# A hybrid decoder trunk in split float32: the order of work at the begin of gate and up, and the outer products of the state update a slab later

## The chip, the cores and the metric

One Trainium2 chip, one core. The metric is device microseconds of one launch, lower is better. Engines are named PE (TensorE), DVE (VectorE), ACT (ScalarE), POOL (GpSimd) and SP (SyncE, which here only issues DMAs).

## What is computed

Two layers (D_MODEL 1024, 512 prompt tokens and 8 sample tokens side by side, float32). Each layer is a mixer and a SwiGLU feed-forward:

```python
h = h + _rmsnorm(m, norm_mix_post[l])
f = _swiglu(_rmsnorm(h, norm_ffn_pre[l]), w_gate_up[l], w_down[l])
h = h + _rmsnorm(f, norm_ffn_post[l])

def _swiglu(hn, w_gate_up, w_down):
    gu = hn @ w_gate_up
    gate, up = jnp.split(gu, 2, axis=-1)
    return (jax.nn.silu(gate) * up) @ w_down
```

The mixer also updates a 128 x 128 state per head for each sample token: new state = decayed state + outer product of key and value (four DeltaNet and four retention heads, 8 sample tokens).

## The kernel before

**Precision.** Each float32 product is done as three products of tensors split in a rounded part (`Xh`, `Wh`, `actH`, made by ACT, `hi`) and a rest (`Xl`, `Wl`, `actL`, made by DVE as the difference, `lo`). 520 columns (two halves of 256 prompt and 4 sample tokens) lie in two PSUM banks; a pair of banks is a slot.

**Weights** come as slabs of eight 128 x 128 blocks (512 KB) over SP's queue into two `stage` buffers, and are split into three `Wh`/`Wl` buffers. A slab is loaded when the `lo` of two slabs before is done; ACT's `hi` of a slab waits until PE has finished with the one three before.

**Gate and up.** The first five of 22 column blocks of gate and up are ten plain tiles (`T_GU` + 0 to 9; even ones gate, odd ones up; `mm6`, L676), one slab each. Tiles `T_GU` + 0 to 2 are computed interleaved in `first_halves`, the others in a row. A tile starts on PE when its slab is split (`wait_slab`) and the tile two before it has been evacuated by DVE (`wait_tile`, semaphores `tile_free0` and `tile_free1`). DVE's loop over j = 0 to 4 evacuates the gate tile (`gp`, L2476), then the up tile (`up`, L2493), scaling both by the norm's factor `rb`; ACT applies SiLU to `gp` between (L1764); then DVE multiplies (L2496). `lo` of a coming slab stands behind each evacuation.

The other 17 column blocks (`Q`) are done by `strassen(q)`: a 2 x 2 scheme with seven products (`UN`) in place of eight, over four blocks of 128 each, with three matmuls per block and product (L1231 to L1233), 84 in all. It needs
- the activations once per layer: `weighted(k)` (ACT, L1706, eight times, two at a time into `XF`), `x_scaled(0..3)` (DVE, L2389, times `rb`), `x_sum(0..3)` (DVE, L2397), `x_high(0..6)` (ACT, L1710), `x_low(0..6)` (DVE, L2401);
- a set of weights per q (`loC`/`hiC`/`fullC` for q = 0, then B and A in turns): four quarters of 256 KB by SP (`quarters`, into `raw12`, `raw1`, `raw21`), `w_sums13`, `w_sum2`, `w_sum4` and four rests `w_low` (DVE), four roundings `w_high` (ACT). Rest 12 (`W_LO12`) is the last that the first product `UA11` waits for, `W_LO46` is waited for by the fifth, `US3`, which also waits for `post(q, U2)` (L2443), one of five small DVE steps that combine products.

These steps were spread by hand over DVE's and ACT's loops of the ten tiles. The scalings 0 and 1 stand at the end of j = 0, ahead of the evacuation of tile `T_GU` + 2; 2 and 3 stand in j = 1 ahead of the evacuation of `T_GU` + 3; the set for q = 0 is made in j = 4 and behind it. Nearly all of these steps count up one semaphore, `ffn_rest`, in program order.

**Down.** 22 slabs, eight tiles of 22 blocks each. After slab 0 PE transposes keys and values of the sample tokens back to rows (`rows_back`); DVE copies them (L2568, L2569) and builds 16 value blocks (`value_block(u)`, L2369); PE makes the outer product `outer(u)` (L1197) after a slab; DVE adds it to the decayed state (`new_state(u)`), which POOL has loaded into one of two `dst` buffers and stores afterwards (`load_state`, `store_state`, in POOL's queue in order). Every engine works its queue in order; what is written behind a wait waits with it.

Of the kernel before, what the change touches and what calls it, by code (L numbers as in the profile page):

```python
# [8 lines left out]
def trunk(nc, xT, w_slabs, w_ba, w_rows, dt_bias, a_log, conv_hist, state_gdn, state_ret, c_f32, c_rope,  # L9
# [7 lines left out]
    P = 128  # L17
# [52 lines left out]
    X_STEPS, XR_STEPS = 8 + UN, KT + UN  # L70
    REST, ROUND = X_STEPS + Q * W_STEPS, XR_STEPS + Q * 4

# [27 lines left out]
    with ctx:  # L100
# [285 lines left out]
        def heads_of(i):  # L386
# [22 lines left out]

            "b1_loaded b12_loaded b21_loaded p_done post_done ffn_rest ffn_round gate_half "  # L410

# [68 lines left out]
        def _(sp):  # L480
# [14 lines left out]
            def quarters(l, q):  # L495

                N = l * Q + q
                used = l * REST + X_STEPS + (q - 1) * W_STEPS
                if q == 0:
                    sp.wait_ge(s["rb_ready"], (l * 4 + 3) * 2)  # L500
                else:
                    sp.wait_ge(s["ffn_rest"], used + W_T13)
                sp.dma_start(raw12[:], quarter(l, q, 1, 0)).then_inc(s["b12_loaded"], 16)
                if q == 0:
                    sp.wait_ge(s["dr_mm"], (l + 1) * 16)
                else:
                    sp.wait_ge(s["ffn_rest"], used + W_LO05)
                sp.dma_start(raw1[:, 0], quarter(l, q, 0, 0)).then_inc(s["b1_loaded"], 16)
                sp.dma_start(raw1[:, 1], quarter(l, q, 1, 1)).then_inc(s["b1_loaded"], 16)
                if q == 0:  # L510
                    last = S_DN - 1 - (l * SLABS + S_DN - 1 - (NW - 1)) % NW
                    sp.wait_ge(s["tile_done"], l * TILES + T_GU + last - S_GU + 1)
                else:
                    sp.wait_ge(s["ffn_rest"], used + W_LO3)
                sp.dma_start(raw21[:], quarter(l, q, 0, 1)).then_inc(s["b21_loaded"], 16)
# [65 lines left out]
        def _(pool):  # L581
# [13 lines left out]
            for l in range(DEPTH):  # L595
# [59 lines left out]
                pool.wait_ge(s["dr_mm"], (l + 1) * 16)  # L655
                pool.wait_ge(s["ffn_rest"], l * REST + X_STEPS + (Q - 1) * W_STEPS + W_LO05)
                load_state(l, 0, False)
# [12 lines left out]
        def _(pe):  # L670
# [53 lines left out]
            for l in range(DEPTH):  # L724
# [474 lines left out]
                def strassen(q):  # L1199
# [4 lines left out]
                    for u, bank in enumerate((a_, b_, c_, a_, b_, c_, d_)):  # L1204
                        if q == 0:
                            pe.wait_ge(s["ffn_rest"], l * REST + 8 + u + 1)
                        if u == UA11:
                            pe.wait_ge(s["ffn_rest"], l * REST + X_STEPS + q * W_STEPS + W_LO12)
                            if q == 0:
# [8 lines left out]
                        elif u == US1 and q >= 2:  # L1218
                            pe.wait_ge(s["post_done"], (N - 2) * POSTS + C12)
                        elif u == UA12:  # L1220
                            pe.wait_ge(s["gate_half"], N * HALVES + P1_COPY)
                        elif u == US3:
                            pe.wait_ge(s["ffn_rest"], l * REST + X_STEPS + q * W_STEPS + W_LO46)
# [32 lines left out]
                for i in range(KT - 1):  # L1256
                    wait_tile(l, T_DN + i)
                    for j in range(FT):
# [36 lines left out]
        def _(act):  # L1295
# [16 lines left out]
            for l in range(DEPTH):  # L1312
# [395 lines left out]
                def x_high(u):  # L1708
                    act.wait_ge(s["ffn_rest"], l * REST + (1, 7, 5, 4, 6, 8, 4)[u])
                    A(XU[:, u, 0], x_full(u), ACT.Copy).then_inc(s["ffn_round"], 1)  # L1710

                def w_high(q, c):

                    N = l * Q + q
                    lo_, hi_, full = w_set(q)
                    rest = l * REST + X_STEPS + q * W_STEPS
                    if c == W_HI05:
# [5 lines left out]
                    elif c == W_HI12:  # L1723
                        act.wait_ge(s["ffn_rest"], rest + W_T2)
                        to, src = hi_[:, US2:US1 + 1], full[:, US2:US1 + 1]
                    else:
                        act.wait_ge(s["ffn_rest"], rest + W_T4)
                        to, src = hi_[:, US3:UA22 + 1:2], full[:, US3:UA22 + 1:2]
# [31 lines left out]
                for j in range(NP):  # L1760
# [101 lines left out]
        def _(dve):  # L1862
# [12 lines left out]
            for l in range(DEPTH):  # L1875
# [508 lines left out]
                def x_scaled(i):  # L2384
# [3 lines left out]
                    dve.wait_ge(s["ffn_round"], l * ROUND + (4 if i < 2 else KT))  # L2388
                    V.tensor_tensor(to, to, rb[:, a:a + 1].to_broadcast([P, 4, HC]), ALU.mult).then_inc(s["ffn_rest"], 1)  # L2389

                def x_sum(i):
# [3 lines left out]
                                          (US2, x_full(US1), x_full(UA11), ALU.subtract, 5), (US4, x_full(UA12), x_full(US2), ALU.add, 7))[i]  # L2395
                    dve.wait_ge(s["ffn_rest"], l * REST + need)
                    V.tensor_tensor(x_full(to), x, y, op).then_inc(s["ffn_rest"], 1)  # L2397

                def x_low(u):
                    dve.wait_ge(s["ffn_round"], l * ROUND + KT + u + 1)  # L2400
                    V.tensor_tensor(XU[:, u, 1], x_full(u), plain(XU[:, u, 0]), ALU.subtract).then_inc(s["ffn_rest"], 1)  # L2401

                def w_sums13(q):
# [4 lines left out]
                    dve.wait_ge(s["b1_loaded"], (N + 1) * 32)  # L2408
                    V.tensor_tensor(full[:, US1:US3 + 1:2], raw1[:], raw12[:].unsqueeze(1).to_broadcast([P, 2, QW]), ALU.add).then_inc(s["ffn_rest"], 1)

                def w_sum2(q):
                    full = w_set(q)[2]
                    dve.wait_ge(s["ffn_rest"], l * REST + X_STEPS + q * W_STEPS + W_T13)
                    V.tensor_tensor(full[:, US2], full[:, US1], raw1[:, 1], ALU.add).then_inc(s["ffn_rest"], 1)

                def w_sum4(q):
                    full = w_set(q)[2]
                    dve.wait_ge(s["b21_loaded"], (l * Q + q + 1) * 16)
                    dve.wait_ge(s["ffn_rest"], l * REST + X_STEPS + q * W_STEPS + W_T2)
                    V.tensor_tensor(full[:, UA22], full[:, US2], raw21[:], ALU.add).then_inc(s["ffn_rest"], 1)  # L2420

                def w_low(q, c):
# [5 lines left out]
                    else:  # L2428
                        us = slice(US2, US1 + 1) if c == W_HI12 else slice(US3, UA22 + 1, 2)
                        src = full[:, us]  # L2430
                        dve.wait_ge(s["ffn_rest"], l * REST + X_STEPS + q * W_STEPS + W_T4)
                    dve.wait_ge(s["ffn_round"], l * ROUND + XR_STEPS + q * 4 + c)
                    V.tensor_tensor(lo_[:, us], src, plain(hi_[:, us]), ALU.subtract).then_inc(s["ffn_rest"], 1)

# [37 lines left out]
                for j in range(NP):  # L2472
# [91 lines left out]
                for i in range(KT * FT // 8 - NW):  # L2564
                    lo(G0 + S_DN + i + NW)
                    if i == 1:
                        dve.wait_ge(s["row_T"], l + 1)
                        step.go(V.tensor_copy(flat2(krows[:]), PS[0:3 * H * NB, 6, 0:2 * P]))  # L2568
                        step(V.tensor_copy(flat2(vrows[:]), PS[0:3 * H * NB, 6, 2 * P:4 * P]))  # L2569
                    if 1 <= i < 17:  # L2570
                        value_block(i - 1)
                    for k in range(KT - 2):
                        if (FT * k + FT - 1) // 8 == i:
                            down_tile(k)
                    if 2 <= i < 18:
                        new_state(i - 2)
                down_tile(KT - 2)
# [146 lines left out]
```

## Time and profile before

| | |
|---|---|
| median of 3 runs | 1404.09 us (1403.06 to 1404.29) |
| profiled execution | 1401.79 us, span 1400.0 us |
| PE busy | 1366.9 us (98%), 12172 matmuls |
| DVE busy | 1040.2 us (74%) |
| ACT busy | 634.9 us (45%) |
| POOL busy | 100.7 us (7%) |
| share of the chain that ended last | PE 83%, DVE 10%, ACT 3% |
| mean granted clock of PE | 0.996 |

Busy shares are averages over the whole span; what a reordering is worth is read from the single waits of PE, in the timeline. Times in the timelines count from the span's start. Durations of back-to-back matmuls overlap, so the start of the next is the better clock for PE, as it is for DVE. Layer 1 repeats layer 0 some 695.2 us later.

### The profile page before, as it was taken

How to read it: one execution, taken by the hardware profiler on the slowest of the kernel's cores; microseconds unless marked ns; L12 is line 12 of the kernel's file. 1: busy time of each engine (PE TensorE's matmuls, PEld its weight loads, DVE VectorE, ACT ScalarE, POOL GpSimd, SP SyncE). 2: the span in 40 equal slices, each digit the busy share in tenths (PEclk: the TensorE clock that was granted, in tenths of full speed). 3: DMA queues.
4: the chain of work that ended last, by engine and by line, in shares of the span. 5: the costliest groups of instructions: out<-in, count | busy, mean ns of one | idle time of the engine just before them, and what ended most of it. 6: DMA issues, size and time to landing. Idle time of an engine off the chain costs nothing.

```text
span 1400.0 us, 29086 instructions
## 1 busy us (share of the span) xinstructions
PE 1366.9 (98%) x12172; PEld 1343.3 (96%) x12172; DVE 1040.2 (74%) x1675; ACT 634.9 (45%) x1230; POOL 100.7 (7%) x141
## 2 busy tenths in 40 slices
PE   8999999999999999999999999999998999999997
PEld 8999999998999999999989999999988999999996
DVE  7746896867888888754586568958778888886554
ACT  5135554557445455422442364634574445454222
POOL 0001211000000000011000012210000000000110
PEclk9999999999999999999999999999999999999999
DMA  6322232022222322354313312421212232323552
GB/s 207 111 102 76 85 115 98 32 79 79 98 99 99 113 99 104 124 181 181 114 61 118 110 62 84 130 69 46 89 69 92 99 113 98 114 95 140 173 180 77
DMA packets 67491, 147.46 MB, mean 105 GB/s; under 512 B 20128, under 2 KB 23584, under 8 KB 67360
## 3 DMA queue, kind: packets, MB, share of 16 engines
q1 hardware_dynamic: 59536, 119.90, 25.2%
q0 software_dynamic: 7824, 25.70, 5.3%
q8 instruction: 96, 1.57, 0.5%
q14 instruction: 35, 0.29, 0.1%
HBM read 132.79 MB, written 12.78 MB: 104 GB/s over the span
## 4 chain that ended last, share of the span: by engine, by line
PE 83%; DVE 10%; ACT 3%; issue 2%; DMA 1%; SPq 0%; DVEq 0%; ACTq 0%
PE PS L676 43%; PE PS L1231 8%; PE PS L1232 8%; PE PS L1233 8%; PE PS L682 5%; DVE Wl L1873 2%; DVE hT L1911 1%; ACT Wh L1310 1%; DVE Xl L1890 1%; ACT XF L1706 1%; DVE actL L2467 1%; ACT actH L1756 1%; DVE mT L1910 1%; PE PS L870 1%; PE PS L1197 1%
## 5 line engine op out<-in xcount | busy, mean ns | idle before, releaser
L1310 ACT ACTIVATE Wh<-stage 128x1024 fp32r<-128x1024 f32 x143 | 151.0, 1058 | 327.1 <-PE PS L676 300.3
L676 PE MATMUL PS<-Xh,Wh 128*128 128x260 f32 x1376 | 285.7, 289 | 7.5 <-DVE sqb L2493 2.7
L676 PE MATMUL PS<-Xh,Wl 128*128 128x260 f32 x1376 | 276.9, 283 | 0.0
L676 PE MATMUL PS<-Xl,Wh 128*128 128x260 f32 x1376 | 276.5, 282 | 0.0
L1873 DVE TENSOR_TENSOR Wl<-stage,Wh 128x1024 fp32r<-128x1024 f32 x143 | 174.5, 1222 | 102.8 <-ACT Wh L1310 102.1
L676 PEld LDWEIGHTS PS<-Xh,Wh 128*128 128x128 f32 x1376 | 211.4, 189 | 11.6 <-issue 6.8
L676 PEld LDWEIGHTS PS<-Xh,Wl 128*128 128x128 f32 x1376 | 211.8, 188 | 0.0
L676 PEld LDWEIGHTS PS<-Xl,Wh 128*128 128x128 f32 x1376 | 211.7, 188 | 0.0
L1231 PE MATMUL PS<-XU,hiA 128*128 128x260 f32 x448 | 126.8, 283 | 0.0
L1231 PE MATMUL PS<-XU,hiB 128*128 128x260 f32 x448 | 126.8, 283 | 0.0
L1232 PE MATMUL PS<-XU,hiB 128*128 128x260 f32 x448 | 126.6, 283 | 0.0
L1232 PE MATMUL PS<-XU,hiA 128*128 128x260 f32 x448 | 126.6, 283 | 0.0
L1233 PE MATMUL PS<-XU,loB 128*128 128x260 f32 x448 | 126.4, 282 | 0.0
L1233 PE MATMUL PS<-XU,loA 128*128 128x260 f32 x448 | 126.4, 282 | 0.0
L676 PE MATMUL PS<-actH,Wh 128*128 128x260 f32 x616 | 124.0, 282 | 0.0
L676 PE MATMUL PS<-actL,Wh 128*128 128x260 f32 x616 | 124.0, 282 | 0.0
L676 PE MATMUL PS<-actH,Wl 128*128 128x260 f32 x616 | 123.9, 282 | 0.0
L676 PEld LDWEIGHTS PS<-actH,Wh 128*128 128x128 f32 x616 | 97.2, 188 | 1.4
L676 PEld LDWEIGHTS PS<-actL,Wh 128*128 128x128 f32 x616 | 94.8, 188 | 0.0
L676 PEld LDWEIGHTS PS<-actH,Wl 128*128 128x128 f32 x616 | 94.8, 188 | 0.0
L1232 PEld LDWEIGHTS PS<-XU,hiA 128*128 128x128 f32 x448 | 84.7, 189 | 0.0
L1232 PEld LDWEIGHTS PS<-XU,hiB 128*128 128x128 f32 x448 | 84.7, 189 | 0.0
(384 smaller groups left out, 2875.1 us busy)
## 6 DMA issues: line engine op xcount, KB each, us to landing
stage<-w_slabs SPq DMA_DIRECT2D x143, 512.0 KB, 3.3
raw<-w_slabs SPq DMA_DIRECT2D x136, 256.0 KB, 2.6
dst<-state_ret POOLq DMA_DIRECT2D x32, 256.0 KB, 3.6
dst<-state_gdn POOLq DMA_DIRECT2D x32, 256.0 KB, 3.8
out_gdn_sample<-dst POOLq DMA_DIRECT2D x16, 256.0 KB, 3.0
out_ret_sample<-dst POOLq DMA_DIRECT2D x16, 256.0 KB, 3.3
hT<-x_t SPq DMA_DIRECT2D x3, 520.0 KB, 6.6
out_y_t<-hT SPq DMA_DIRECT2D x3, 520.0 KB, 3.0
```

The source lines that it names most:

```text
L676: ins = mm(pj(slot)[:, a], w[:, ws, pos, :], x[:, a, :], start=first and w is Wh and x is xh, stop=last and w is Wl)
L682: ins = mm(pj(slot)[:, a], w[:, ws, pos, :], x[:, a, :], start=first and w is Wh and x is xh, stop=last and w is Wl)
L870: ins = mm(PS[rows, 7, B_U:B_U + P], vectors, dst[:, u % 2, j, :], start=n == 0, stop=n == 7 and u < 8, skip_group_check=True)
L1197: mm(PS[:, 4 + u % 2, :], krows[:, u // 8, :], vblks[u % 2].rearrange("p a n -> p (a n)"), start=True, stop=True).then_inc(s["outer_mm"], 1)
L1231: mm(PS[:, bank, 0:HC], hi_[:, u, cols], XU[:, u, 0, k], start=k == 0 and u in (UA11, US2, US1, UA22), stop=False, skip_group_check=True)
L1232: mm(PS[:, bank, 0:HC], hi_[:, u, cols], XU[:, u, 1, k], start=False, stop=False, skip_group_check=True)
L1233: ins = mm(PS[:, bank, 0:HC], lo_[:, u, cols], XU[:, u, 0, k], start=False, stop=k == 3, skip_group_check=True)
L1310: A(Wh[:, G % NW], stage[:, G % NS], ACT.Copy).then_inc(s["hi_split"], 1)
L1706: A(to, hT[:, k], ACT.Copy, scale=prm[:, l, row:row + 1]).then_inc(s["ffn_round"], 1)
L1756: A(actH[:, j:j + n], actF[:, j:j + n] if j < FT - 2 else act_full(j).unsqueeze(1), ACT.Copy).then_inc(s["ah_ready"], n)
L1873: V.tensor_tensor(Wl[:, G % NW], stage[:, G % NS], Wh[:, G % NW].bitcast(fp32), ALU.subtract).then_inc(s["lo_split"], 1)
L1890: V.scalar_tensor_tensor(Xl[:, k, a], hT[:, k, a], prm[:, layer, row:row + 1], Xh[:, k, a].bitcast(fp32), ALU.mult, ALU.subtract).then_inc ...
```

## The change

In gate and up, on DVE: `x_scaled(0)` and `(1)` move from the end of j = 0 to j = 1 behind the evacuation of tile `T_GU` + 2 (and `lo`); `x_scaled(2)` and `(3)` move behind the evacuation of `T_GU` + 3; sums and `x_low` follow later by about half a round. `w_sums13(0)` and `w_sum2(0)` move to the end of j = 3; the rests 05, 3 and 12, `w_sum4(0)` and `x_low(6)` move ahead of the evacuation of the last plain tile, only rest 46 stays behind it. On ACT: `w_high(0, W_HI05)` and `w_high(0, W_HI3)` with the wait for `state_stored` move from behind the loop into j = 3, behind `x_high`. As steps of activations and of weights are now interleaved in another order, `ffn_rest` is split into `xu_rest` (activations) and `w_rest` (weights), with the counts adapted at every wait, SP's and POOL's too. In down, row copies, value blocks, outer products and state additions come one slab later.

```diff
-    REST, ROUND = X_STEPS + Q * W_STEPS, XR_STEPS + Q * 4
+    REST, ROUND = Q * W_STEPS, XR_STEPS + Q * 4
...
-                        elif b % 8 == 7 and 2 <= b // 8 < 18:
-                            outer(b // 8 - 2)
+                        elif b % 8 == 7 and 3 <= b // 8 < 19:
+                            outer(b // 8 - 3)
...
                     if j == 3:
                         for u in range(3, UN):
                             x_high(u)
-                act.wait_ge(s["state_stored"], (l + 1) * 32)
-                for c in range(W_HI05, W_HI46 + 1):
-                    w_high(0, c)
+                        act.wait_ge(s["state_stored"], (l + 1) * 32)
+                        w_high(0, W_HI05)
+                        w_high(0, W_HI3)
+                w_high(0, W_HI12)
+                w_high(0, W_HI46)
...
                     if j == 1:
-                        x_scaled(2)
-                        x_scaled(3)
+                        x_scaled(0)
+                        x_scaled(1)
                     elif j == 2:
+                        x_sum(1)
                         x_sum(2)
-                        x_sum(3)
                     elif j == 3:
                         x_low(2)
                         x_low(3)
                     elif j == 4:
-                        w_sums13(0)
-                        w_sum2(0)
                         w_low(0, W_HI05)
+                        w_sum4(0)
+                        w_low(0, W_HI3)
+                        w_low(0, W_HI12)
+                        x_low(6)
                     done(t + 1)
                     freed(V.tensor_tensor(up, pj(1), rb[:], ALU.mult), t + 1)
...
-                    if j == 0:
-                        x_scaled(0)
-                        x_scaled(1)
-                    elif j == 1:
+                    if j == 1:
+                        x_scaled(2)
+                        x_scaled(3)
                         x_sum(0)
-                        x_sum(1)
                     elif j == 2:
+                        x_sum(3)
                         x_low(0)
                         x_low(1)
                     elif j == 3:
-                        for u in range(4, UN):
-                            x_low(u)
+                        x_low(4)
+                        x_low(5)
+                        w_sums13(0)
+                        w_sum2(0)
                     elif j == 4:
-                        w_sum4(0)
-                        w_low(0, W_HI3)
-                        w_low(0, W_HI12)
                         w_low(0, W_HI46)
...
-                    if i == 1:
+                    if i == 2:
                         dve.wait_ge(s["row_T"], l + 1)
...
-                    if 1 <= i < 17:
-                        value_block(i - 1)
+                    if 2 <= i < 18:
+                        value_block(i - 2)
...
-                    if 2 <= i < 18:
-                        new_state(i - 2)
+                    if 3 <= i < 19:
+                        new_state(i - 3)
```

## Rows read from the trace of the kernel before

**Rows 1.** Waits of PE, whole run: who waited for whom, us in total, times, longest

```profile
PE PS L1231 <- DVE loC L2433: 7.8, 2, 3.9
PE PS L676 <- DVE sqb L2493: 2.7, 4, 1.2
PE PS L676 <- DVE sqb L2476: 2.2, 2, 1.1
...
PE PS L1197 <- DVE vblk L2369: 0.8, 2, 0.4
```

**Rows 2.** Timeline of PE: start us, us, engine, line, operation [idle before <- releaser]

```profile
341.10 0.48 PE L676 MATMUL PS<-Xh,Wh 128*128 128x260 f32 x2 [0.20 <-DVE sqb L2493]
...
348.18 0.47 PE L676 MATMUL PS<-Xh,Wh 128*128 128x260 f32 x2 [1.12 <-DVE sqb L2476]
...
355.32 0.47 PE L676 MATMUL PS<-Xh,Wh 128*128 128x260 f32 x2 [1.17 <-DVE sqb L2493]
```

**Rows 3.** Timeline of PE, from the last plain tile to the third Strassen block

```profile
383.95 0.40 PE L676 MATMUL PS<-Xh,Wl 128*128 128x260 f32 x2
388.26 0.56 PE L1231 MATMUL PS<-XU,hiC 128*128 128x260 f32 x1 [3.91 <-DVE loC L2433]
...
399.85 0.29 PE L1231 MATMUL PS<-XU,hiB 128*128 128x260 f32 x1
...
409.95 0.29 PE L1231 MATMUL PS<-XU,hiA 128*128 128x260 f32 x1
```

**Rows 4.** Stretches: length, busy us of PE, PEld, DVE, ACT, POOL, PEclk, DMA share, GB/s

```profile
384.40:388.26 3.86, 0.00 (x0) 0.03 (x1) 3.83 (x6) 1.80 (x2) 0.00 (x0) 0.95 0.17 55
388.26:391.40 3.14, 3.14 (x15) 3.14 (x16) 3.11 (x4) 0.36 (x2) 0.00 (x0) 0.52 0.20 78
1083.40:1087.60 4.20, 4.20 (x22) 4.20 (x23) 3.99 (x4) 2.04 (x4) 0.00 (x0) 0.60 0.33 117
```

**Rows 5.** Timeline of DVE at the first plain tiles of layer 0

```profile
345.03 2.39 DVE L2389 TENSOR_TENSOR XF<-XF,rb 128x1040 f32<-128x1040 f32 x2 [1.26 <-ACT XF L1706]
347.35 0.69 DVE L2476 TENSOR_TENSOR sqb<-PS,rb 128x520 f32<-128x520 f32 x1
...
352.17 2.39 DVE L2389 TENSOR_TENSOR XF<-XF,rb 128x1040 f32<-128x1040 f32 x2 [3.00 <-ACT XF L1706]
354.48 0.69 DVE L2493 TENSOR_TENSOR sqb<-PS,rb 128x520 f32<-128x520 f32 x1
```

**Rows 6.** Timeline of DVE behind the last plain tile of layer 0

```profile
384.39 0.70 DVE L2493 TENSOR_TENSOR sqb<-PS,rb 128x520 f32<-128x520 f32 x1 [2.08 <-PE PS L676]
385.12 0.70 DVE L2496 TENSOR_TENSOR actF<-sqb 128x520 f32<-128x520 f32 x1
385.74 0.68 DVE L2420 TENSOR_TENSOR fullC<-fullC,raw 128x512 f32<-128x512 f32 x1
...
386.94 2.35 DVE L2433 TENSOR_TENSOR loC<-fullC,hiC 128x1024 fp32r<-128x1024 f32 x2
389.21 1.22 DVE L2409 TENSOR_TENSOR fullB<-raw,raw 128x1024 f32<-128x1024 f32 x1
390.46 0.69 DVE L2414 TENSOR_TENSOR fullB<-fullB,raw 128x512 f32<-128x512 f32 x1
391.07 1.22 DVE L2433 TENSOR_TENSOR loB<-raw,hiB 128x1024 fp32r<-128x1024 f32 x1
```

**Rows 7.** The tiles `raw`, whole run: time of their loads

```profile
DMA to landing us min/median/max: 2.5/2.6/4.9
```

**Rows 8.** Timelines of DVE and of PE at the first outer product of layer 0

```profile
578.01 0.42 DVE L2568 CAST krows<-PS 96x256 fp32r<-96x256 f32 x1
...
578.79 0.69 DVE L2369 TENSOR_TENSOR vblk<-vrows,cf 96x512 fp32r<-96x512 f32 x1
581.88 1.22 DVE L1873 TENSOR_TENSOR Wl<-stage,Wh 128x1024 fp32r<-128x1024 f32 x1 [2.40 <-ACT Wh L1310]
...
579.53 0.50 PE L1197 MATMUL PS<-vblk,krows 96*128 96x512 f32 x1 [0.40 <-DVE vblk L2369]
```

More of the change, by code:

```diff
@@ L408, in trunk @@
             "cm_ready x_zeroed mtk_ready dkl_ready kd_ready s_decayed "
-            "b1_loaded b12_loaded b21_loaded p_done post_done ffn_rest ffn_round gate_half "
+            "b1_loaded b12_loaded b21_loaded p_done post_done xu_rest w_rest ffn_round gate_half "
             "dve_step act_step").split()
@@ L497, in quarters @@
                 N = l * Q + q
-                used = l * REST + X_STEPS + (q - 1) * W_STEPS
+                used = l * REST + (q - 1) * W_STEPS
                 if q == 0:
@@ L501, in quarters @@
                 else:
-                    sp.wait_ge(s["ffn_rest"], used + W_T13)
+                    sp.wait_ge(s["w_rest"], used + W_T13)
                 sp.dma_start(raw12[:], quarter(l, q, 1, 0)).then_inc(s["b12_loaded"], 16)
@@ L506, in quarters @@
                 else:
-                    sp.wait_ge(s["ffn_rest"], used + W_LO05)
+                    sp.wait_ge(s["w_rest"], used + W_LO05)
                 sp.dma_start(raw1[:, 0], quarter(l, q, 0, 0)).then_inc(s["b1_loaded"], 16)
@@ L513, in quarters @@
                 else:
-                    sp.wait_ge(s["ffn_rest"], used + W_LO3)
+                    sp.wait_ge(s["w_rest"], used + W_LO3)
                 sp.dma_start(raw21[:], quarter(l, q, 0, 1)).then_inc(s["b21_loaded"], 16)
@@ L655, in _ @@
                 pool.wait_ge(s["dr_mm"], (l + 1) * 16)
-                pool.wait_ge(s["ffn_rest"], l * REST + X_STEPS + (Q - 1) * W_STEPS + W_LO05)
+                pool.wait_ge(s["w_rest"], l * REST + (Q - 1) * W_STEPS + W_LO05)
                 load_state(l, 0, False)
@@ L1205, in strassen @@
                         if q == 0:
-                            pe.wait_ge(s["ffn_rest"], l * REST + 8 + u + 1)
+                            pe.wait_ge(s["xu_rest"], l * X_STEPS + 8 + u + 1)
                         if u == UA11:
-                            pe.wait_ge(s["ffn_rest"], l * REST + X_STEPS + q * W_STEPS + W_LO12)
+                            pe.wait_ge(s["w_rest"], l * REST + q * W_STEPS + W_LO12)
                             if q == 0:
@@ L1222, in strassen @@
                         elif u == US3:
-                            pe.wait_ge(s["ffn_rest"], l * REST + X_STEPS + q * W_STEPS + W_LO46)
+                            pe.wait_ge(s["w_rest"], l * REST + q * W_STEPS + W_LO46)
                             pe.wait_ge(s["post_done"], N * POSTS + U2)
@@ L1708, in x_high @@
                 def x_high(u):
-                    act.wait_ge(s["ffn_rest"], l * REST + (1, 7, 5, 4, 6, 8, 4)[u])
+                    act.wait_ge(s["xu_rest"], l * X_STEPS + (1, 7, 5, 4, 6, 8, 4)[u])
                     A(XU[:, u, 0], x_full(u), ACT.Copy).then_inc(s["ffn_round"], 1)
@@ L1715, in w_high @@
                     lo_, hi_, full = w_set(q)
-                    rest = l * REST + X_STEPS + q * W_STEPS
+                    rest = l * REST + q * W_STEPS
                     if c == W_HI05:
@@ L1723, in w_high @@
                     elif c == W_HI12:
-                        act.wait_ge(s["ffn_rest"], rest + W_T2)
+                        act.wait_ge(s["w_rest"], rest + W_T2)
                         to, src = hi_[:, US2:US1 + 1], full[:, US2:US1 + 1]
                     else:
-                        act.wait_ge(s["ffn_rest"], rest + W_T4)
+                        act.wait_ge(s["w_rest"], rest + W_T4)
                         to, src = hi_[:, US3:UA22 + 1:2], full[:, US3:UA22 + 1:2]
@@ L2388, in x_scaled @@
                     dve.wait_ge(s["ffn_round"], l * ROUND + (4 if i < 2 else KT))
-                    V.tensor_tensor(to, to, rb[:, a:a + 1].to_broadcast([P, 4, HC]), ALU.mult).then_inc(s["ffn_rest"], 1)
+                    V.tensor_tensor(to, to, rb[:, a:a + 1].to_broadcast([P, 4, HC]), ALU.mult).then_inc(s["xu_rest"], 1)
                 def x_sum(i):
@@ L2395, in x_sum @@
                                           (US2, x_full(US1), x_full(UA11), ALU.subtract, 5), (US4, x_full(UA12), x_full(US2), ALU.add, 7))[i]
-                    dve.wait_ge(s["ffn_rest"], l * REST + need)
-                    V.tensor_tensor(x_full(to), x, y, op).then_inc(s["ffn_rest"], 1)
+                    dve.wait_ge(s["xu_rest"], l * X_STEPS + need)
+                    V.tensor_tensor(x_full(to), x, y, op).then_inc(s["xu_rest"], 1)
                 def x_low(u):
                     dve.wait_ge(s["ffn_round"], l * ROUND + KT + u + 1)
-                    V.tensor_tensor(XU[:, u, 1], x_full(u), plain(XU[:, u, 0]), ALU.subtract).then_inc(s["ffn_rest"], 1)
+                    V.tensor_tensor(XU[:, u, 1], x_full(u), plain(XU[:, u, 0]), ALU.subtract).then_inc(s["xu_rest"], 1)
                 def w_sums13(q):
@@ L2408, in w_sums13 @@
                     dve.wait_ge(s["b1_loaded"], (N + 1) * 32)
-                    V.tensor_tensor(full[:, US1:US3 + 1:2], raw1[:], raw12[:].unsqueeze(1).to_broadcast([P, 2, QW]), ALU.add).then_inc(s["ffn_rest"], 1)
+                    V.tensor_tensor(full[:, US1:US3 + 1:2], raw1[:], raw12[:].unsqueeze(1).to_broadcast([P, 2, QW]), ALU.add).then_inc(s["w_rest"], 1)
                 def w_sum2(q):
                     full = w_set(q)[2]
-                    dve.wait_ge(s["ffn_rest"], l * REST + X_STEPS + q * W_STEPS + W_T13)
-                    V.tensor_tensor(full[:, US2], full[:, US1], raw1[:, 1], ALU.add).then_inc(s["ffn_rest"], 1)
+                    dve.wait_ge(s["w_rest"], l * REST + q * W_STEPS + W_T13)
+                    V.tensor_tensor(full[:, US2], full[:, US1], raw1[:, 1], ALU.add).then_inc(s["w_rest"], 1)
                 def w_sum4(q):
@@ L2418, in w_sum4 @@
                     dve.wait_ge(s["b21_loaded"], (l * Q + q + 1) * 16)
-                    dve.wait_ge(s["ffn_rest"], l * REST + X_STEPS + q * W_STEPS + W_T2)
-                    V.tensor_tensor(full[:, UA22], full[:, US2], raw21[:], ALU.add).then_inc(s["ffn_rest"], 1)
+                    dve.wait_ge(s["w_rest"], l * REST + q * W_STEPS + W_T2)
+                    V.tensor_tensor(full[:, UA22], full[:, US2], raw21[:], ALU.add).then_inc(s["w_rest"], 1)
                 def w_low(q, c):
@@ L2430, in w_low @@
                         src = full[:, us]
-                        dve.wait_ge(s["ffn_rest"], l * REST + X_STEPS + q * W_STEPS + W_T4)
+                        dve.wait_ge(s["w_rest"], l * REST + q * W_STEPS + W_T4)
                     dve.wait_ge(s["ffn_round"], l * ROUND + XR_STEPS + q * 4 + c)
-                    V.tensor_tensor(lo_[:, us], src, plain(hi_[:, us]), ALU.subtract).then_inc(s["ffn_rest"], 1)
+                    V.tensor_tensor(lo_[:, us], src, plain(hi_[:, us]), ALU.subtract).then_inc(s["w_rest"], 1)
                 def post(q, n):
```

## The prediction

> **What bounds the kernel now.** I read the page's first part, then the waits of TensorE (PE), then the timeline of PE around each of them. PE is busy 98% of the span, so only its idle stretches and its slow ones can be won. The list of its waits [rows 1] shows the same few in both layers: 7.8 us in two equal waits of the first outer-scheme product (L1231) for the weight rests `loC` (L2433), 4.9 us in six short ones of the plain tiles (L676) for the two evacuations (L2476, L2493; each layer also has one of 0.2 us that stays), and 0.8 us in two waits of the outer products (L1197) for `vblk`. I call the ten plain gate and up tiles 1 to 10 (`T_GU` + 0 to 9), and their slabs likewise. In layer 0, tile 4 starts at 341.10, tile 5 at 348.18 and tile 6 at 355.32 [rows 2]; tiles 6 to 10 then run without a gap up to 383.95 + 0.24 = 384.19 (two matmuls are left in that row), which is 28.87 / 5 = 5.77 us a tile; Strassen block 0 starts at 388.26, block 1 at 399.85, block 2 at 409.95 [rows 3]. A block without waits is thus 10.10 us, and block 0 took 11.59. The extra 1.49 us is the clock: after the idle stretch the granted clock is 0.52 from 388.26 to 391.40, near the lower level of 1.2 GHz, against 0.95 in the idle stretch ahead, and in layer 1 it is 0.60 over 1083.40 to 1087.60, which has some full-speed matmuls at its begin [rows 4]. From tile 4 to block 1 the stretch is 58.75 us; without waits it would be 7 x 5.77 + 10.10 = 50.49. So 8.26 us per layer lie here: 1.3 + 1.4 in front of tiles 5 and 6, 4.1 in front of block 0, 1.5 in clock.
>
> **Gate and up, first half: the scalings.** VectorE (DVE) finishes the first two `x_scaled` at 345.03 + 2.39, and only then evacuates tile 3 (347.35), which tile 5 waits for; the next two begin at 352.17, because they wait for ScalarE's (ACT's) eighth `weighted`, and the evacuation of tile 4 (354.48), which tile 6 waits for, stands behind them [rows 5]. The change moves no instruction out: four scalings, four sums, seven rests, all still there. It puts the first evacuation directly behind `lo` of slab 5, and the second behind `x_scaled(0)` and `(1)`, whose `weighted` ended at 345.0, when DVE's idle time on them ended [rows 5]. My walk: `lo` of slab 5 ends at 343.8, where DVE's idle 1.26 us ahead of 345.03 began; tile 3 is evacuated 0.62 later, at 344.4. Slab 6 is rounded by ACT behind the four `weighted`, about one pass (1.1 us, my estimate from DVE's passes over a tensor of that size) after 345.0; its rest follows to 347.2, two scalings to 349.5, tile 4 is evacuated at 350.2. PE wants these at 346.9 (tile 5) and 352.7 (tile 6). Both waits go, with 2.5 us of margin each. What is late next is nothing of PE's: `x_scaled(2)`, `(3)` and the sums now run from 352 to 360 behind evacuations of tiles that finished earlier, and tile n+2 needs an evacuation only one whole tile, 5.77 us, after tile n ends. By the durations, DVE has some 4.1 and 5.9 us of work per half of rounds j = 1 and 2 against 5.77 us a tile; the second halves exceed it, the pair does not.
>
> **First weight set.** Before, behind the evacuation of tile 10 stood `act` (0.73 after it began), then `w_sum4` (0.62 later), rests 3 and 12, and only then could PE start: 384.39 to the end of the first of the two rests that begin at 386.94 [rows 6]. The change does `w_sums13`, `w_sum2` in j = 3 and rests 05, `w_sum4`, 3, 12 and `x_low(6)` ahead of tile 10's evacuation. Does it fit? Round j = 3, second half: evacuation with `act` 0.73 + 0.62, two `x_low` of 1.15 (a tensor of 1040 takes 2.38 to 2.39 in pairs, overlapped [rows 5]), `w_sums13` 1.25, `w_sum2` 0.61 [rows 6]: 5.5 against 5.77. Round j = 4, first half: 0.62 + 1.14 + 0.60 + 0.60 + 1.14 + 1.15 = 5.25 against 5.77. Rest 12 is ready near 380.2, block 0 starts at 341.10 + 7 x 5.77 = 381.5: 1.3 us of margin, so the 4.1 us go whole. On ACT, the wait for `raw21` now stands ahead of the fifth SiLU. That load starts when tile 8 ends and lands in 2.5 to 4.9 us [rows 7], a tile later SiLU is due: the wait is hidden, at worst by 0.9 us. SP issues the same loads in the same order, a few us earlier; the split of the semaphore adds none that blocks.
>
> **A new wait behind it.** Block 0's fifth product (US3) needs `post(0, U2)`, and on DVE seven instructions stand between the end of tile 10 and the end of that: evacuation 0.73, `act` 0.62, the last rest 1.14, `w_sums13(1)` 1.25, `w_sum2(1)` 0.61, rest 05 of set 1 1.14 (pitches [rows 6]), `U2` itself some 0.45, the step from PE's end to DVE 0.2 and back to PE 0.12: 6.26 us after block 0's start. PE is there after 4/7 x 10.10 = 5.77. It waits 0.49 us. Before, this was covered by the slow clock. The trace of before does not show this wait; its bounds are 0 (if the last rest slips ahead) and 1.2 (the longest short wait of a tile [rows 1]); I take 0.49, from the pitches of just these instructions.
>
> **Clock.** The low stretch follows each of the two waits of 3.9 us and none of those of 1.1 and 1.2 us, whose tiles run on at full pace [rows 2, 4]. With the long wait gone I take the 1.5 us back entirely; bounds 0 and 1.6. The Trainium skill, "TensorE: Matmul & The Clock Gate", Part 1, says that the default state is throttled, that activity releases it, and that the ramp varies from run to run; the trace agrees in so far as layer 1's low stretch began later behind its wait than layer 0's.
>
> **DVE's pace.** In the rows a next instruction starts 0.08 to 0.1 us before the one ahead has ended (389.21 + 1.22 with a successor at 390.46 is the exception, a dependent one; 390.46 + 0.69 has it at 391.07) [rows 6]. Against this change speaks the Trainium skill, "VectorE: DVE Perf Modes", The DRAIN you can't avoid: the next op "does not start until the 8-stage pipe empties". By that, each of the some seven steps would cost 0.08 us more, the wait at US3 would be 1.0 and not 0.49, and the total 1 us less; the rows decide, and they have the overlap.
>
> **Outer products a slab later.** Same work: 16 products, 16 blocks, two row copies per layer, each one slab of 8 blocks later on PE, DVE and through POOL's queue of state loads and stores. Now `vblk` is 0.4 us late for the first product at 579.53. Later, DVE starts `lo` at 581.88, 1.13 after it the copies, and these with the block took 578.01 to 579.48, 1.47 us: ready at 584.5 [rows 8]. PE reaches the product 5.77 after 579.13, at 584.9. The wait goes, margin 0.4: 0.4 us per layer (bounds 0 and 0.5). At the end of down the last `new_state` stands ahead of the evacuation of tile 7 of 8, where nothing is due before the first half of the last tile ends (66 matmuls at 10.10 / 84 = 0.12 us each, 7.9 us); hidden. POOL's last store and the reload of `rope` move 6 us later, still well ahead of their users: the next layer's projection, or the end of the run.
>
> **Sum.** Per layer 8.26 - 0.49 = 7.77; two layers 15.5; down 0.8; together 16.3 us. The profiled execution of 1401.79 us would become 1385.5. It lies 2.3 us under the median of the runs, 1404.09, so the median after is 1387.8.
>
> **Rivals.**
> A, the clock does not come back: a low stretch of the same length remains in each layer, behind the shorter waits. For: the fall in layer 1 came 1 us after PE had started again, so it is not tied to the wait alone. Against: none follows the 1.1 us waits. Price 2 x 1.5: 1390.8. Chance 0.07.
> B, DVE's queue runs late: the two halves of 5.5 and 5.25 us have margins of 0.3 and 0.5 only, and behind them every us goes straight into the wait at US3. At 0.1 us more per instruction, some twelve in a row, 1.2 us per layer: 1390.2. Chance 0.12.
> C, the change does only half of what it says: tile 6 now waits for slab 6's rests, because ACT rounds that slab behind the four `weighted`, or for the evacuation behind two scalings. For: the order is so. Against: margins of 5 and 2.5 us. Price 2.7 x 2: 1393.2. Chance 0.03.
> D, slower: ACT, an in-order queue, sits at `w_high(0, HI3)` for `raw21` ahead of the fifth SiLU. If the load landed later than 5.8 us behind tile 8's end, each further us would delay SiLU, `act`, the last rest and block 0. It costs more than the whole gain from a landing of some 14 us; the longest in the trace is 4.9 [rows 7]. A landing of 16 us would give 1404.09 + 2 x 2 = 1408. Chance 0.02.
>
> **How the numbers follow.** The forecast has 0.76: 1387.8, its own range 1385.5 (US3 without wait, 1 us of scatter between runs) to 1390 (US3 at 1.2, the 0.4 of down not won). With A and B on top, low 1385.5, high 1392.5; C's and D's shares and a little below stay out. About 0.2%, 2.8 us, is what a measurement of this kernel can tell from no change. Faster 0.96: the forecast, A, B and C all lie over 10 us below 1404, less a rest; same 0.02; slower 0.02, D.
>
> **What would show it.** In the profile after: no wait of L676 for L2476 or L2493 beyond the 0.2 us one; no wait of L1231 for `loC`; granted clock 1.00 in block 0; a new short wait, about 0.5 us, of a product for `rb` (L2443's successor); from tile 4 to block 1 some 51.0 us; no wait of the outer product for `vblk`. The prediction is wrong if block 0 still begins behind a wait, or if blocks 1 to 3 show waits that blocks in the steady part do not.

## The result, and the profile after

| | before | after |
|---|---|---|
| median of 4 runs | 1404.19 us (1403.06 to 1405.91) | 1384.49 us (1384.18 to 1384.63) |
| profiled execution | 1401.79 us | 1384.18 us |
| mean granted clock of PE | 0.996 | 0.998 |

The ratio is 0.9858, 95% interval 0.9841 to 0.9875: 19.7 us faster, against the 16.3 forecast, and 1.0 us under the low end of the range (1385.5). Between the two profiled executions the gain is 17.6 us.

Waits of PE after, whole run (us in total, times, longest; lines lie two to four later than before, from L1873 on):

```profile
PE PS L676 <- DVE Xl L1934: 2.2, 2, 1.3
...
PE PS L1231 <- DVE rb L2445: 0.7, 2, 0.3
...
PE PS L676 <- DVE sqb L2497: 0.4, 2, 0.2
```

The waits of [rows 1] are gone but for the two of 0.2 us ahead of tile 4, and one new kind stands there, for `rb` (L2445, which is `post(0, U2)`).

Timelines after, DVE at the first plain tiles, then at the last one (columns as in [rows 5]):

```profile
342.65 1.22 DVE L1875 TENSOR_TENSOR Wl<-stage,Wh 128x1024 fp32r<-128x1024 f32 x1 [0.18 <-ACT Wh L1310]
343.80 0.69 DVE L2478 TENSOR_TENSOR sqb<-PS,rb 128x520 f32<-128x520 f32 x1
346.08 1.22 DVE L1875 TENSOR_TENSOR Wl<-stage,Wh 128x1024 fp32r<-128x1024 f32 x1 [1.59 <-ACT Wh L1310]
347.23 2.38 DVE L2391 TENSOR_TENSOR XF<-XF,rb 128x1040 f32<-128x1040 f32 x2
349.53 0.69 DVE L2497 TENSOR_TENSOR sqb<-PS,rb 128x520 f32<-128x520 f32 x1
...
379.03 1.22 DVE L2435 TENSOR_TENSOR loC<-fullC,hiC 128x1024 fp32r<-128x1024 f32 x1
380.17 1.23 DVE L2403 TENSOR_TENSOR XU<-XF,XU 128x1040 fp32r<-128x1040 f32 x1
381.84 0.70 DVE L2497 TENSOR_TENSOR sqb<-PS,rb 128x520 f32<-128x520 f32 x1 [0.44 <-PE PS L676]
382.58 0.70 DVE L2500 TENSOR_TENSOR actF<-sqb 128x520 f32<-128x520 f32 x1
383.19 1.22 DVE L2435 TENSOR_TENSOR loC<-fullC,hiC 128x1024 fp32r<-128x1024 f32 x1
```

Tile 3 is evacuated at 343.80 in place of 347.35 [rows 5], tile 4 at 349.53 in place of 354.48; rest 12 begins at 379.03 and is ready before the last tile ends, where it stood behind it in [rows 6]. The stretches of the seven tiles and of block 0 (columns as in [rows 4]):

```profile
341.20:381.64 40.44, 40.44 (x336) 40.44 (x337) 36.90 (x38) 24.36 (x30) 0.00 (x0) 1.00 0.35 109
1027.00:1067.44 40.44, 40.44 (x336) 40.44 (x337) 36.90 (x38) 24.35 (x30) 0.00 (x0) 1.00 0.33 110
381.64:385.60 3.96, 3.96 (x36) 3.96 (x35) 3.69 (x5) 1.86 (x3) 0.00 (x0) 1.00 0.05 21
385.60:392.29 6.69, 6.36 (x54) 6.18 (x52) 6.59 (x10) 2.67 (x4) 0.00 (x0) 1.00 0.51 159
```

Seven tiles run without a gap at full clock (40.44 us, 40.39 forecast), block 0 takes 10.65 us with its one wait, in place of 11.59 in [rows 3]. The wait itself:

```profile
387.89 0.36 PE L1231 MATMUL PS<-XU,hiC 128*128 128x260 f32 x1 [0.33 <-DVE rb L2445]
```

The whole run can be cut in five at points that the chain of work names in each profile: the begin, the first matmul of the second half's norm sums (L712), the begin of the last down tile (L682, 69 matmuls), and the same two in layer 1. Lengths in us, worked out from those starts:

| profile | begin | gate, up, down 0 | middle | gate, up, down 1 | end |
|---|---|---|---|---|---|
| before | 336.99 | 340.12 | 354.97 | 340.23 | 27.69 |
| after | 337.09 | 331.78 | 354.02 | 331.79 | 27.72 |
| before, second profile (e1) | 337.83 | 341.20 | 354.36 | 340.03 | 27.68 |

### The profile page after: what moved, and what is told of

It is laid out like the page before. It is cut to its first block, busy times and chain, and to the rows that moved or that the text cites. A ratio compares the mean times of both kernels' runs of the same rounds, so it can differ in the third digit from the quotient of the medians.

```text
span 1382.4 us, 29088 instructions
## 1 busy us (share of the span) xinstructions
PE 1362.3 (99%) x12172; PEld 1339.7 (97%) x12172; DVE 1039.6 (75%) x1675; ACT 634.8 (46%) x1230; POOL 100.5 (7%) x141
## 4 chain that ended last, share of the span: by engine, by line
PE 88%; DVE 8%; ACT 1%; issue 1%; DMA 1%; SPq 0%; DVEq 0%; ACTq 0%
PE PS L676 48%; PE PS L1231 8%; PE PS L1232 8%; PE PS L1233 8%; PE PS L682 5%; DVE Wl L1875 1%; DVE hT L1913 1%; DVE Xl L1892 1%; DVE mT L1912 1%; PE PS L870 1%; DVE conv L2002 1%; PE PS L1197 1%; PE PS L1016 1%; PE PS L842 1%; PE PS L854 1%
```

## The experiments

Two questions were open: where 19.7 - 16.3 us come from, and whether the low clock hangs on the idle stretch of PE. Theory A: my sum is right for the execution that was profiled, and the rest is a cost of the removed waits that this execution happened not to pay in full. Rival B: the change wins something that my sum does not have, in down above all.

**e1, the kernel before once more.**

> The kernel before, unchanged, to see how its executions differ. The profiled execution of before took 1401.79 us and its other runs 1403.06 to 1405.91; the changed kernel's runs lie within 0.45 us. Theory A (the part of the gain beyond my sum is a matter of which execution of before was profiled): ratio 1.000, runs spread over 2 us or more, a profile that has other stalls than the first, in the granted clock or in PE's issue, worth 1 to 3 us; the mean granted clock of the longer runs is lower than 0.996. Rival B (the change itself wins some 3 us that my sum has not): runs of before differ only by chance under 1 us and the profile repeats the first one, stall for stall.

Measured: 1403.73 us (1402.11 to 1405.92, 11 runs) beside 1402.73 (1400.62 to 1406.58, 26 runs) of the same code, ratio 1.0007 (0.9998 to 1.0016). The spread is as theory A wants it. The longest run, 1405.92, has the lowest mean clock, 0.991; the two with 0.995 took 1402.11 and 1402.54. The clock does not order all runs: among the 26 beside it, one with 0.995 took 1404.69. The profile shows what differs. First profile of before, then this one, stretches at block 0:

```profile
386.00:388.00 2.00, 0.00 (x0) 0.00 (x0) 2.00 (x3) 1.54 (x2) 0.00 (x0) 0.97 0.00 0
388.00:390.00 2.00, 1.74 (x8) 1.77 (x9) 2.00 (x3) 0.46 (x1) 0.00 (x0) 0.50 0.39 131
390.00:392.00 2.00, 2.00 (x14) 2.00 (x14) 1.97 (x3) 0.76 (x2) 0.00 (x0) 0.67 0.23 82
392.00:394.00 2.00, 2.00 (x19) 2.00 (x18) 1.51 (x4) 1.09 (x2) 0.00 (x0) 1.00 0.41 150
```

```profile
388.00:390.00 2.00, 0.86 (x4) 0.89 (x5) 2.00 (x2) 1.34 (x2) 0.00 (x0) 0.50 0.37 128
390.00:392.00 2.00, 2.00 (x11) 2.00 (x11) 1.97 (x4) 0.00 (x0) 0.00 (x0) 0.50 0.01 3
392.00:394.00 2.00, 2.00 (x11) 2.00 (x10) 1.17 (x2) 1.85 (x3) 0.00 (x0) 0.50 0.40 131
394.00:396.00 2.00, 2.00 (x16) 2.00 (x15) 1.28 (x3) 0.00 (x0) 0.00 (x0) 0.82 0.74 257
```

Behind the same wait of 3.91 us the clock is at 0.50 (1.2 GHz) to about 391.3 in one execution and to about 394.7 in the other. The longer one costs the stage 1.08 us more (341.20 against 340.12). The execution of before that I had was the cheapest kind: short in both layers, clock 0.996, where the runs here have 0.991 to 0.995.

**e2, the outer products alone.** Edit of the kernel before:

```diff
-                        elif b % 8 == 7 and 2 <= b // 8 < 18:
-                            outer(b // 8 - 2)
+                        elif b % 8 == 7 and 3 <= b // 8 < 19:
+                            outer(b // 8 - 3)
...
-                    if i == 1:
+                    if i == 2:
...
-                    if 1 <= i < 17:
-                        value_block(i - 1)
+                    if 2 <= i < 18:
+                        value_block(i - 2)
...
-                    if 2 <= i < 18:
-                        new_state(i - 2)
+                    if 3 <= i < 19:
+                        new_state(i - 3)
```

> The kernel before with only the outer products, value blocks, row copies and state additions a slab later. Theory A: the two waits of 0.4 us for vblk go and nothing else, 0.8 us, ratio 0.9994, at most 1.2 us. Rival B (the unexplained 3 us come from down): 3 to 4 us, ratio 0.9975.

Measured: 1402.68 us (1401.18 to 1404.01, 11 runs), ratio 0.9998 (0.9989 to 1.0007). The interval reaches from 1.5 us less to 1.0 us more, so it is not the 3 us of rival B; whether 0 or 1 us the time can't tell under the clock's spread. The profile can: no wait for `vblk`, and gate, up and down 0, with the short low stretch as in the first profile of before, take 339.61 us against 340.12. Layer 1 had the long stretch here (340.80).

**e3, gate and up alone.** The changed kernel with the four edits of e2 undone.

> The changed kernel with the outer products back where they were, so only gate and up is changed. Theory A: 0.8 us more than the changed kernel (1384.5), 1385.3 us, and two waits of 0.4 us for vblk in the profile. Rival B (down holds the rest): 1387 to 1388 us.

Measured: 1386.78 us (1386.06 to 1389.06, 4 runs), ratio 0.989 (0.9876 to 0.9903). The time lies just under rival B's band (1387 to 1388) and 1.5 us over theory A's 1385.3, so it doesn't decide; the profile does, for theory A's mechanism: no wait of 3.9 us, and gate, up and down take 332.47 and 332.46 us, 0.68 more per layer than after, and the begin 338.54 in place of 337.09, as here the clock fell in the first tile:

```profile
10.00:12.00 2.00, 0.91 (x4) 0.92 (x5) 1.73 (x3) 2.00 (x4) 0.00 (x0) 0.76 0.99 397
12.00:14.00 2.00, 2.00 (x11) 2.00 (x11) 2.00 (x4) 2.00 (x4) 0.00 (x0) 0.50 1.05 399
```

0.68 and not 0.40 per layer is what the outer products' shift wins in this comparison (e2 has 0.51 in layer 0). The profile's 0.40 is counted from the modelled end of the matmul before; from start to start a wait costs more, as the tiles' 1.12 and 1.17 us cost 1.3 and 1.4.

**e4, the wait filled.** The kernel before with work for PE where it waited:

```diff
+                for _ in range(8):
+                    mm(PS[:, 7, 0:HC], ones, cf[:, 0:HC], start=True, stop=True)
                 for q in range(Q):
                     strassen(q)
```

> The kernel before with eight float32 matmuls over constants (3.5 us, into a PSUM bank that block 0 overwrites before it is read) ahead of the first Strassen block, so that PE is busy in the stretch in which it waits for the weight rests. The order on DVE and ACT stays. Theory A (the low clock of block 0 comes from the 3.9 us of idle PE): block 0 starts when it did, the granted clock in it is 1.00 and it takes 10.1 us in place of 11.6, 3 us in all, 1401.2 us. Rival (the low clock comes from the place, or from the kind of work, not from the idle stretch): block 0 stays at 11.6 us, no gain, 1404.2 us.

Measured: 1398.97 us (1398.25 to 1401.71, 9 runs), ratio 0.9973 (0.9964 to 0.9983). The timeline of PE, the filler, the first matmul of block 0 and the first of the block after:

```profile
384.71 3.67 PE L1253 MATMUL PS<-cf 128*128 128x260 f32 x16
388.79 0.36 PE L1231 MATMUL PS<-XU,hiC 128*128 128x260 f32 x1 [0.41 <-DVE loC L2435]
399.03 0.29 PE L1231 MATMUL PS<-XU,hiB 128*128 128x260 f32 x1
```

And the stretch behind the filler, in which the granted clock (third number from the end) stays at 1.00:

```profile
388.50:392.00 3.50, 3.21 (x26) 3.24 (x27) 3.47 (x5) 1.68 (x4) 0.00 (x0) 1.00 0.24 78
```

Block 0 takes 10.24 us. Nothing on DVE or ACT was moved, PE did more work, and the kernel is 3.8 us faster: the low clock hangs on PE's idle stretch. By the medians it costs 3.8 us in both layers together; the interval, 2.4 to 5.0, holds the 3.0 that I read from one profile too. The profiles agree with both: gate, up and down take 338.78 and 338.80 us here, 2.8 less than in the first profile of before, which had two short stretches, and 3.7 less than in e1's, which had a short and a long one.

**e5, the weight set back in its place.** The changed kernel with `w_high`, `w_sums13`, `w_sum2`, rests 3, 12 and `w_sum4` of set 0, and `x_low(6)`, where before had them (rest 05 stands ahead of the last evacuation in both kernels; what the change took from in front of it are the two sums):

```diff
-                        act.wait_ge(s["state_stored"], (l + 1) * 32)
-                        w_high(0, W_HI05)
-                        w_high(0, W_HI3)
+                act.wait_ge(s["state_stored"], (l + 1) * 32)
+                w_high(0, W_HI05)
+                w_high(0, W_HI3)
...
                     elif j == 4:
+                        w_sums13(0)
+                        w_sum2(0)
                         w_low(0, W_HI05)
-                        w_sum4(0)
-                        w_low(0, W_HI3)
-                        w_low(0, W_HI12)
-                        x_low(6)
...
-                        w_sums13(0)
-                        w_sum2(0)
+                        x_low(6)
                     elif j == 4:
+                        w_sum4(0)
+                        w_low(0, W_HI3)
+                        w_low(0, W_HI12)
                         w_low(0, W_HI46)
```

> The changed kernel with the first weight set made where it was before, behind the evacuation of the last plain tile; scalings, sums and the outer products stay as changed. Theory A: the two tile waits stay away (1.3 and 1.4 us per layer), the outer product wins 0.68 per layer, but the wait of 3.9 us for loC is back and with it the low clock, now in its typical and not in its shortest length: about 6.7 us better than before, some 12.5 us worse than the changed kernel, and runs that again spread over 2 us or more. Rival (the low clock has another cause): the spread stays under 1 us.

Measured: 1396.46 us (1394.68 to 1399.5, 5 runs) beside 1402.74 of before on the same chip, ratio 0.9955 (0.9942 to 0.9968): 6.3 us better than before, 11.4 worse than the changed kernel (e8), the wait of 3.9 us back in each layer and the spread with it, 4.8 us. The forecast had 6.7 and 12.5. In the profile the clock fell behind both waits, for the long stretch in layer 0 (337.70 us) and the short one in layer 1 (336.74). So both parts of the change in gate and up do what the forecast said of them.

**e6, a wait of middle length.** The changed kernel with `w_low(0, W_HI12)` moved behind the last evacuation:

```diff
-                        w_low(0, W_HI12)
                         x_low(6)
                     elif j == 4:
+                        w_low(0, W_HI12)
                         w_low(0, W_HI46)
```

> The changed kernel with one step, rest 12, moved back behind the evacuation of the last plain tile. Block 0 then waits 0.73 + 0.62 + 1.15 and start-up, 2.6 us per layer, between the 1.2 us that no low clock follows and the 3.9 us that it always follows. The wait at US3 falls away. If the clock does not fall: 2 x 2.2 = 4.4 us over the changed kernel, spread under 1 us. If it falls as behind the long wait: 7.5 to 10 us over it, and a spread of 2 us or more.

Measured: 1392.37 us (1391.41 to 1393.54, 5 runs), 7.4 us over e8, at the edge of the 7.5 to 10 that a fallen clock was to cost and far from the 4.4 without one. The clock falls here too, though not before block 0 has started. Its first matmul in the timeline of PE:

```profile
384.57 0.36 PE L1231 MATMUL PS<-XU,hiC 128*128 128x260 f32 x1 [2.71 <-issue]
```

The stretches around it:

```profile
384.00:386.00 2.00, 1.43 (x8) 1.46 (x9) 2.00 (x3) 0.00 (x0) 0.00 (x0) 0.76 0.00 0
386.00:388.00 2.00, 2.00 (x11) 2.00 (x10) 1.97 (x3) 0.83 (x3) 0.00 (x0) 0.50 0.04 6
388.00:390.00 2.00, 2.00 (x16) 2.00 (x16) 1.34 (x3) 1.02 (x2) 0.00 (x0) 0.89 0.51 158
```

(In this profile the wait on `loC` is put down to "issue"; rest 12 is what it waited for, by the edit.) So 2.7 us of idle PE was enough in both layers, and a rest that is 1.1 us long costs 3.7 us per layer by the medians (3.9 in the profiles, where gate, up and down take 335.76 and 335.69 us) when it falls on the wrong side of PE's last tile. Its stretches of low clock are short in both layers, and the spread is 2.1 us.

**e7, the new wait taken out.** In the changed kernel:

```diff
+                        if q == 0:
+                            post(q, U2)
                         w_low(q + 1, W_HI05)
                         if q:
                             gated(q - 1)
-                        post(q, U2)
+                            post(q, U2)
```

> The changed kernel with post(0, U2) ahead of rest 05 of the next set for block 0. The wait at US3 (0.33 us in each layer, some 0.5 with the start of the queue) goes, as U2 is ready 1.1 us earlier: 0.9 us less than the changed kernel, about 1383.6. Rival: DVE's queue is late by then in any case, and the wait comes back at another product of block 0 or at block 1: no gain.

Measured: 1385.29 us (1383.21 to 1385.53, 4 runs) beside 1385.02 of the changed kernel: the times show no gain. The profile shows it: no wait for `rb`, and gate, up and down take 331.23 and 331.27 us in place of 331.82 and 331.82, 0.57 per layer. It is hidden by the begin: three of the four runs have a mean clock of 0.996, and the profiled one was low in its first tile. Run by run at the same mean clock it shows: 1383.21 with 0.998, where e8 has 1383.82 and 1383.84, and 1385.09 to 1385.53 with 0.996, where e8 has 1386.2 and 1386.9.

**e8, the changed kernel again, and e10, a third time.**

> The changed kernel, unchanged, beside the others on the same chip. Theory A (the spread of before, 1400.6 to 1406.6, is the length of the low clock behind the 3.9 us waits, which are gone here): runs within 1 us of each other except where the clock is low at the begin of the kernel, mean granted clock 0.997 or 0.998, ratio to before 0.986 to 0.988. In the profile the small 32 x 32 matmuls of layer 1 (L992) show at most 0.2 us of issue stall; if the 0.9 us lost there in the first profile of before was chance, some profile of the changed kernel can show it too.

> The changed kernel once more, for comparison with the version with post(0, U2) early and the filled begin, on the same chip. As before: two kinds of runs, near 1384 with a mean clock of 0.998 and near 1386 to 1387 with 0.996, when the clock falls at the begin; gate, up and down of either layer take 331.8 us in the profile, 8.3 to 8.4 us less than in the first profile of before.

Measured: e8 1385.02 us (1383.82 to 1386.9, 4 runs), ratio 0.9874 (0.986 to 0.9887); e10 1384.92 (1383.06 to 1386.96, 4 runs), ratio 0.987 (0.9856 to 0.9883). Gate, up and down are 331.82, 331.82 and 331.99, 331.80. e8's spread goes with the mean clock: two runs near 1383.8 with 0.998, two at 1386.2 and 1386.9 with 0.996, and in the profiled one of these the clock fell at the begin. In e10 the 0.998 runs alone reach from 1383.06 to 1385.29, which the clock does not explain. Over the three comparisons the change wins 17.7 to 19.7 us.

**e9, a version that beats both.** e7, and a little of the warm-up that the kernel already has (L730) where the first tile waits for its input:

```diff
+                            if u == 0 and k in (1, 2):
+                                for _ in range(k):
+                                    mm(PS[:, 7, 0:2 * P], zeros[:, 0, :], flat2(zeros[:]), start=True, stop=True)
                             pe.wait_ge(s["x_ready"], 2 * k + 2)
```

> The kernel with post(0, U2) early, and with one and two of the warm-up matmuls over zeros ahead of the second and the third step of the very first tile, where PE waits for the input's transfers and where in some executions the clock then falls (seen in three profiles of kernels without the long waits). Theory A (a low clock comes from PE's idle time wherever it is): no low clock before the end, mean clock 0.998 in all runs, spread under 1 us, 1383.2 to 1383.6 us against 1384 to 1387 of the changed kernel. Rival: the low clock at the begin stays in half of the runs, or the added matmuls delay the first tile by up to 2 us: 1385 or more.

Measured: 1381.83 us (1381.6 to 1382.47, 5 runs), ratio to before 0.9848 (0.9835 to 0.9862), 3.1 us less than e10 on the same chip, with a spread of 0.9 us where e10 has 3.9. The mean clock is 0.997 or 0.998 in all five, and in the profile it does not fall at the begin; the other four have no profile, and e10's profiled run had 0.997 with the clock low at the begin, so that it stayed high there in all five is likely by the spread, not shown. The gain is more than expected: 1.1 us of it is US3, and the middle stage takes 352.68 us where the other profiles of changed kernels have 354.01 to 354.23. No edit of e9 aims at that 1.3 us; see the last section.

## Why the prediction was right and wrong

**Right: the mechanisms, and for the profiled execution nearly the sizes.** The tile waits: forecast away, they are away; evacuations at 344.4 and 350.2 forecast, finished at 344.5 and 350.2. Rest 12 ready "near 380.2": 380.2. Seven tiles in 40.39 us: 40.44. The wait at US3: 0.49 forecast; block 0 takes 0.55 more than a block without waits, and e7 wins 0.57 by removing it. The wait of ACT for `raw21` is hidden, the evacuation of tile 10 has its margin (0.44 us, forecast 0.5). None of the four rivals occurred. On DVE's pace the rows held: the steps start 0.08 us ahead of the end of the one before here too (379.03 + 1.22 with a successor at 380.17). The sentence of the Trainium skill ("VectorE: DVE Perf Modes", The DRAIN you can't avoid) that the prediction set against this does not hold for these steps: by it the wait at US3 would have been 1.0 us. The same section goes on that a next op that is not held starts earlier, which the prediction left out and with which the trace agrees.

**The step that failed** is the last sentence of the sum: "It lies 2.3 us under the median of the runs, 1404.09, so the median after is 1387.8." It takes the distance between profile and median as something that the change leaves alone. It was not: after the change the distance is 0.3 us, which is 2.0 of the 3.3 us missed. About half of the 2.0 is the thing that the change removes: the low clock behind the 3.9 us waits has different lengths from run to run, and the profile had the short one in both layers. One long stretch more costs 1.1 us (e1), and the filled wait (e4) puts the two layers at 3.8 together in the medians. The clock's own term, "the 1.5 us back entirely; bounds 0 and 1.6" per layer, was read from two samples of one execution and shares that fault: behind the long stretch of e1 block 0 takes 2.55 us more than a block without waits. The other half is which runs the first comparison drew, and no experiment gives it a cause: before has medians of 1402.73, 1402.74 and 1403.27 in the later comparisons, and not 1404.19, and the changed kernel 1385.02 and 1384.92, and not 1384.49. The small distance after is chance as well: the profiled runs of e8 and e10 lie 1.2 and 2.0 us over their medians, behind a low clock at the begin. The range's low end allowed 1 us for scatter between runs, on top of a distance taken as fixed. The Trainium skill's remark in "TensorE: Matmul & The Clock Gate", Part 1, that the ramp varies from run to run was in the prediction, and e1 shows it, but I drew no width from it.

The other 1.3 us, between the profiles: 0.55 is the outer product's wait, mis-sized as 0.40 per layer where e3 has 0.68, since I had corrected the tiles' waits for start to start and this one not. 0.95 is the middle stage, 354.97 us in before's profile and 354.02 after; 0.1 us each at the begin and in gate and up go against it. In that stage the profile of before has one idle stretch of 0.68 us, put down to issue, in the small 32 x 32 matmuls (L992) of layer 1. In seven other profiles (after, e1, e4, e5, e7, e8, e10) such a stretch of 0.2 to 0.7 us lies in layer 0, and in four there is none; so it is no work of the change. What makes it was not found.

The statement that the low clock is tied to the long wait alone ("none of those of 1.1 and 1.2 us") holds, but I had no wait between those and 3.9 us to read from: 2.7 us was enough ahead of block 0 (e6).

## What to carry to other kernels

The distance between a profiled execution and the median of the runs is a measurement too: where the change removes something that varies, such as the clock behind a long wait, compare the mean clocks of all runs first, and give the forecast the width of their spread. A wait of PE can cost more than its length, here 3.8 us on top of two of 3.9 us; filling it with throw-away matmuls (e4) is a cheap test of how much. When steps are moved out of the way of the bound engine, a single step of 1.1 us left on the wrong side of the last tile (e6) cost 7.4 of the 17.7 us that all of them won together.

## What the runs showed that I had not expected

**A memset on POOL holds a copy on DVE.** Profile of after, POOL and DVE in the middle stage, then the same two in e9 (its lines lie three later):

```profile
882.53 1.81 POOL L644 MEMSET XT<- 128x2048 f32 x1 [23.50 <-PE PS L945]
...
883.00 1.36 DVE L1996 COPY raw<-histT 128x24 f32<-128x24 f32 x1
```

```profile
882.38 1.81 POOL L644 MEMSET XT<- 128x2048 f32 x1 [22.10 <-PE PS L948]
...
881.92 0.17 DVE L1999 COPY raw<-histT 128x24 f32<-128x24 f32 x1
```

The copy takes 0.17 us where it runs alone and 1.36 where it began inside the memset; it ends at 884.36, the memset at 884.34. It is so in all eleven profiles other than e9's: the copy begins 0.2 to 0.5 us inside this memset, takes 1.3 to 1.6 us and ends within 0.05 us of its end. A subtraction of two tensors (L1878, 1.22 us from 882.12 in e9) ran beside the memset at its usual length, so it is not every DVE instruction that is held. In e9 DVE is 0.9 us earlier against POOL, the copy is over before the memset begins, and PE's wait of 1.1 us for `bv` (L886), which all other profiles have, is not there. That fits the 1.3 us that e9 wins in this stage; the collision alone was not tried, so it is argued, not shown. DVE is earlier there because it waited less for a transfer some 21 us before, the load of `Aq`: 0.73 us in e9, 1.68 in the profile of after, 1.39 to 2.03 in all eleven others. Why `Aq` landed earlier, and whether it did in e9's four runs without a profile, stays open.

**The clock falls at the begin as well**, in five of the twelve profiles (e3, e5, e7, e8, e10), behind waits of PE for the first input (1.8 us for `Xl` and 1.3 for `Wl` in e3, 2.2 and 1.2 in e8, in e5 none over 1.8); where it does, the begin takes 338.5 to 339.6 us in place of 337.0 to 338.1. In e9's profile it does not. Length alone does not decide it: in e2's profile one wait of 2.9 us stands there,

```profile
PE PS L676 <- DVE Xl L1932: 2.9, 1, 2.9
```

and no low clock follows it, where 2.7 us ahead of block 0 was followed by one in both layers of e6. What decides between the two was not tried.
